# The rotary key's block as fp32 matmuls of 32 columns, and 32 bytes more ahead of the stage tensors

## The reference

```python
h = rmsnorm(x, norm_g)                       # x * rsqrt(mean(x*x)) * gain
proj = h @ w_in
(a_b, a_c, a_x, a_z, c_q, c_kv, k_pe, b_z, dq, dk, dv, c_z, gate_pre) = jnp.split(proj, ...)
q  = rmsnorm(c_q, q_a_norm_g) @ w_uq         # c_q 256 columns
kv = rmsnorm(c_kv, kv_a_norm_g) @ w_ukv      # c_kv 128 columns
k  = concat([k_nope, broadcast(k_pe)])       # k_pe: the rotary key, 32 columns
```

## Time and profile before

| | |
|---|---|
| runs, median (lowest, highest) | 1454.65 us (1454.61, 1457.88) |
| profiled execution, its span | 1454.06 us, 1452.3 us |
| PE, PEld busy | 1438.2 us (99%), 1362.6 us (94%) |
| DVE, ACT, POOL busy | 1043.4 us (72%), 852.3 us (59%), 89.7 us (6%) |
| granted clock of TensorE, mean | 0.999 |
| DMA | 291.93 MB, mean 201 GB/s |

### The profile page before, as it was taken

How to read it: one execution, slowest core, us unless ns; L and a number is a source line. 1 busy time by engine, 2 the same in 40 slices (tenths; PEclk the granted TensorE clock), 3 DMA queues, 4 the chain that set the end, 5 groups by cost and what they waited for, 6 DMA issues and landing times.

```text
span 1452.3 us, 30492 instructions
## 1 busy us (share of the span) xinstructions
PE 1438.2 (99%) x11788; PEld 1362.6 (94%) x11788; DVE 1043.4 (72%) x1781; ACT 852.3 (59%) x1482; POOL 89.7 (6%) x144
## 2 busy tenths in 40 slices
PE   8999999999999999999999999999999999999999
PEld 6888999999989999999998989899999898989999
DVE  2888898987685677865675857876676685787664
ACT  4566666555556666545566776665566576665553
POOL 0111011110000000000001000220000100031000
PEclk9999999999999999999999999999999999999999
DMA  9976699996674465766563555336666355434563
GB/s 364 332 215 213 233 333 335 341 342 224 203 231 152 141 193 184 234 193 193 186 225 121 166 160 160 114 122 188 192 193 217 104 173 167 153 105 141 184 197 116
DMA packets 81122, 291.93 MB, mean 201 GB/s; under 512 B 9185, under 2 KB 10465, under 8 KB 80882
## 3 DMA queue, kind: packets, MB, share of 16 engines
q1 hardware_dynamic: 68274, 244.31, 51.3%
q0 software_dynamic: 11728, 42.64, 8.7%
q10 hardware_dynamic: 1008, 3.41, 0.6%
HBM read 289.27 MB, written 1.05 MB: 200 GB/s over the span
## 4 chain that ended last, share of the span: by engine, by line
PE 91%; DVE 4%; ACT 3%; DMA 1%; issue 1%; SPq 0%; DVEq 0%; ACTq 0%
PE G L528 23%; PE G L530 22%; PE G L529 22%; PE G L587 2%; PE G L589 2%; PE G L588 2%; DVE wlo L1735 1%; PE Tp L981 1%; PE O L1139 1%; ACT whi L1201 1%; PE Tp L923 1%; DMA raw<-in_w 1%; PE S L1105 1%; PE S L1034 1%; DVE aw L1743 1%
## 5 line engine op out<-in xcount | busy, mean ns | idle before, releaser
L1735 DVE TENSOR_TENSOR wlo<-raw,whi 128x1024 fp32r<-128x1024 f32 x444 | 544.1, 1228 | 256.3 <-ACT whi L1201 255.1
L1201 ACT ACTIVATE whi<-raw 128x1024 fp32r<-128x1024 f32 x444 | 468.7, 1058 | 222.0 <-PE G L530 168.2
L528 PE MATMUL G<-h,whi 128*128 128x256 f32 x2064 | 582.7, 282 | 0.3 <-DVE wlo L1735 0.2
L529 PE MATMUL G<-h,whi 128*128 128x256 f32 x2064 | 572.0, 277 | 0.0
L530 PE MATMUL G<-h,wlo 128*128 128x256 f32 x2064 | 571.9, 277 | 0.0
L528 PEld LDWEIGHTS G<-h,whi 128*128 128x128 f32 x2064 | 388.3, 188 | 9.6 <-issue 8.4
L529 PEld LDWEIGHTS G<-h,whi 128*128 128x128 f32 x2064 | 388.1, 188 | 0.7 <-issue 0.5
L530 PEld LDWEIGHTS G<-h,wlo 128*128 128x128 f32 x2064 | 387.9, 188 | 0.0
L1743 DVE CUSTOM_DVE_ANT_0 aw<-aw,cs,cols 128x1024 f32<-128x1024 f32 x80 | 101.4, 1279 | 0.0
L528 PE MATMUL G<-ah,whi 128*128 128x256 f32 x352 | 98.5, 280 | 0.0
L529 PE MATMUL G<-ah,whi 128*128 128x256 f32 x352 | 98.5, 280 | 0.0
(11 more groups left out here) (432 smaller groups left out, 2332.2 us busy)
## 6 DMA issues: line engine op xcount, KB each, us to landing
raw<-in_w SPq DMA_DIRECT2D x444, 512.0 KB, 3.9
aw<-in_ada POOLq DMA_DIRECT2D x80, 512.0 KB, 5.3
adaw<-in_ada SPq DMA_DIRECT2D x8, 1024.0 KB, 15.5
sn<-in_uq ACTq DMA_DIRECT2D x2, 768.0 KB, 4.5
x<-in_x SPq DMA_DIRECT2D x1, 1024.0 KB, 5.3
pt<-in_ukv ACTq DMA_DIRECT2D x2, 512.0 KB, 6.1
out<-x SPq DMA_DIRECT2D x4, 256.0 KB, 2.3
dec<-in_dec ACTq DMA_DIRECT2D x1, 512.0 KB, 7.8
```

Source lines behind the costliest of these rows:

```text
L528: pe.matmul(o, wh, mv[:, 0:T], start=(k == 0), stop=False)
L529: pe.matmul(o, wh, mv[:, T:2 * T], start=False, stop=False)
L1201: act.activation(whi[:, s, :], raw[:, s, :], ACT.Copy).then_inc(w_hi, 1)
L1735: dve.tensor_tensor(wlo[:, s, :], raw[:, s, :], whi[:, s, :], ALU.subtract).then_inc(w_lo, 1)
```

## The change

Five edits.

1. Weight blocks 2 and 3 of each hybrid layer change places: block 2 is now k_pe and block 3 is c_kv. The block of k_pe is still fetched whole, 512 KB.
2. ACT and DVE prepare it in another way: ACT copies the 32 used columns of each k tile to `wkp` (128x256), and DVE multiplies by the norm's gains. There is no high and low part.
3. PE computes it in `rotary_block`: eight fp32 matmuls of 32 columns with x itself as moving operand, tile k into partitions 32 (k mod 4) of the result, so in four column groups of the array. It stands between `run_two` and `entry_sums`.
4. The four partial results lie in 128 partitions of `kpT` and are added by `rotary_key`, whose `ident` corner becomes `eye4`, four 32x32 unit matrices one below the other, made once on DVE.
5. `mark` has 40 words, not 32. All that is allotted behind it starts 32 bytes later; so `mh`, `ah`, `yr`, `oh` and `yh` start at multiples of 64, and `cmask`, `ua` and `hpair` no longer do.

```diff
-        mark = sb("mark", [P, HYB_S])
+        mark = sb("mark", [P, 40])
...
+        eye4 = sb("eye4", [P, 32], stack=second)
+        wkp = sb("wkp", [P, T], stack=second)
...
-        kpT = ua[0:32, 2:2 + T]
+        kpT = ua[:, 2:2 + T]
...
+                def rotary_block():
...
+                    b, g = B_HYB + 2, G_HYB + 2
+                    pe.wait_ge(slot_free[(g - 2) % 4], taken(g - 2) + g4)
+                    pe.wait_ge(w_lo, b + 1 + 4 * b4)
+                    for k in range(KT):
+                        c = 32 * (k % 4)
+                        ins = pe.matmul(gslot(g)[c:c + 32, :], wkp[:, 32 * k:32 * k + 32], x[:, k, :],
+                                        start=(k < 4), stop=(k >= 4))
+                    ins.then_inc(blk_done, 1)
...
+                rotary_block()
                 entry_sums()
-                for j in range(2, 8):
+                for j in range(3, 8):
                     block_u(j)
...
-                        ins = pe.matmul(Tp[:, slot, 32 * j:32 * j + 32], kpT[:, j * P:(j + 1) * P], ident[0:32, 0:32],
+                        ins = pe.matmul(Tp[:, slot, 32 * j:32 * j + 32], kpT[:, j * P:(j + 1) * P], eye4[:, :],
...
+                if n in ROTARY:
+                    act.activation(thin(wkp[:, :]), thin_raw(s), ACT.Copy).then_inc(w_hi, 1)
+                    return
...
+                    dve.tensor_tensor(thin(wkp[:, :]), thin(wkp[:, :]), gain.unsqueeze(2).broadcast_to([P, KT, 32]), ALU.mult).then_inc(w_lo, 1)
...
+            chain.link(dve.tensor_reduce(out=eye4[:, :], in_=ident[:, :].rearrange("p (j c) -> p c j", j=4), op=ALU.add,
+                                         axis=AX))
```

More of the change, by code:

```diff
@@ L48 @@
 N_BLOCKS = B_HYB + LAYERS2 * HYB_BLOCKS
+ROTARY = [B_HYB + l * HYB_BLOCKS + 2 for l in range(LAYERS2)]
 G_QKV = 0
@@ L423, in entry_gain, with thin, thin_raw @@
             return cols[:, c:c + 1] if l else gain0[:, k:k + 1]
+        def thin(ap):
+            return ap.rearrange("p (k c) -> p k c", c=32)
+        def thin_raw(s):
+            return raw[:, s, :].rearrange("p (k c) -> p k c", c=P)[:, :, 0:32]
         def first_tile(b):
@@ L1529, in raw_out @@
                     done(j)
-                    dst = cF[:, j, :] if j < 3 else kpT if j == 3 else bz[:, j - 4, :]
+                    dst = (cF[:, 0, :], cF[:, 1, :], kpT, cF[:, 2, :])[j] if j < 4 else bz[:, j - 4, :]
                     src = S[:, 0, 0:T] if j == 1 else gslot(G_HYB + j)
-                    freed(act.activation(dst, src[0:32, :] if j == 3 else src, ACT.Copy), j)
+                    freed(act.activation(dst, src, ACT.Copy), j)
                 def norm_tiles(ks):
@@ L1734, in lo @@
                 dve.wait_ge(w_hi, n + 1 + 4 * r4)
+                if n in ROTARY:
+                    c = C_HYB + LC + L_NORM
+                    gain = cols[:, c:c + KT] if ROTARY.index(n) else gain0
+                    dve.tensor_tensor(thin(wkp[:, :]), thin(wkp[:, :]), gain.unsqueeze(2).broadcast_to([P, KT, 32]), ALU.mult).then_inc(w_lo, 1)
+                    return
                 dve.tensor_tensor(wlo[:, s, :], raw[:, s, :], whi[:, s, :], ALU.subtract).then_inc(w_lo, 1)
@@ L2216, in _ @@
                     dve.wait_ge(slot_free[n % 4], taken(n) + g4)
-                    dst = cF[:, k, :] if k < 3 else kpT
-                    ins = dve.tensor_tensor(dst, dst, rstd[0:32, :] if k == 3 else rstd[:, :], ALU.mult)
+                    dst = (cF[:, 0, :], cF[:, 1, :], kpT, cF[:, 2, :])[k]
+                    ins = dve.tensor_tensor(dst, dst, rstd[:, :], ALU.mult)
                 ins.then_inc(cs_scaled, 1)
@@ L2580, in lay_out @@
         a_b, a_c, a_x, a_z, c_q, c_kv, k_pe, b_z, dq, dk, dv, c_z, gate = (w[:, p:q] for p, q in zip(at[:-1], at[1:]))
-        parts += [blocks(c_q), blocks(c_kv), blocks(np.pad(k_pe, ((0, 0), (0, 96))))]
+        parts += [blocks(c_q), blocks(np.pad(k_pe, ((0, 0), (0, 96)))), blocks(c_kv)]
         parts += [blocks(b_z), blocks(dq, by_tile), blocks(dk, by_tile), token_blocks(dv), blocks(c_z)]
```

## The result

The changed kernel takes 1444.12 us (median of four runs, 1441.61 to 1449.57) against 1454.63 before; ratio 0.9929, interval 0.9909 to 0.995. A second set of six runs gave 1444.63 and 0.9927 (0.9909 to 0.9945). Forecast: 1444.4.

The account below looks back on a forecast made before the run. PE was taken to bound the kernel (busy 1438.2 of 1452.3 us). Terms: -9.9 - 0.7 + 0.3 = -10.3 us, giving 1444.4 us on the median; own range 1441.5 to 1447, with the third and fourth rivals 1440.5 to 1450.0.

Parts of the forecast that it names:

- predicted -9.9 - 0.7: Matmuls on the five moved tensors: 2688 at 3.7 ns less each, 9.9 us, plus 0.7 us on 258-column ones.
- The 0.7 us for matmuls of 258 columns: In `run_unnormed`, 2 x 96 matmuls on slices of `yr` and `ah`: gain of 0 to 0.7 us, taken as 0.7.
- predicted +0.3: Both hybrid entries together: 5.7 us leaving PE paid back as 1.9 us of rotary blocks and about 4 us of waits.
- where X lands: At both entries the rotary block delays the norm's chain: first block on `h` 0.4 us later, then -0.15 in the second layer.
- X: Time of the rotary block's eight fp32 matmuls ahead of the sums, taken as 0.95 us, upper bound 3.3.
- The lower bound of X: Rotary block at its shortest: four rounds of 0.42 / 2, given as 0.86 us.
- My signs of being right: `ah`, `yr`, `mh` windows at 113 to 114 ns; PE waiting at both entries; sums to first `h` block hardly shorter.
- The first: Rival for the five moved tensors: the 32 bytes gain nothing, only the entries change, 1455.5 us; chance 0.13.
- its region: Within the first rival: slow operands lie high in the partition and `h` low, so a memory region would explain them too.
- the single-file column groups: Rival for the rotary block: groups run one after another, 3.3 us, giving 1449.1 or 1460.2 us; chance 0.03.
- The third: Rival for blocks on the moved tensors: DVE's own work turns a third of the gain into waits, 1448 us; chance 0.07.
- The fourth: Rival for the entries: ACT and DVE have more slack, so -3.8 us instead of +0.3, 1440.3 us; chance 0.03.

Follow-up runs that it names:

- e1: The kernel before with only `mark` enlarged to 40 words (edit 5 alone): 1442.05 us, ratio 0.9913.
- e5: The kernel before with `mark` of 48 words, so stage tensors 64 bytes later and still off the multiple of 64: 1455.38 us, ratio 0.999.
- e6: The changed kernel with `h` alone moved 32 bytes off the multiple of 64: 1468.35 us, ratio to the kernel before 1.0076.
- e10: The changed kernel with the rotary block behind the sums and block 4's weight copies ahead of the root: 1438.32 us, ratio to the kernel before 0.987.
- e12: The changed kernel again, unaltered, six more runs: 1444.63 us, ratio to the kernel before 0.9927.
- e9: The changed kernel with the weights `whi` and `wlo` moved 32 bytes off the multiple of 64: 1477.1 us, ratio to the kernel before 1.0134.
- e2: The changed kernel with `mark` back at 32 words (edits 1 to 4 alone): 1455.38 us, ratio to the kernel before 1.0003.
- e7: The changed kernel with all eight fp32 matmuls of the rotary block in one column group: 1449.66 us, ratio to the kernel before 0.9976.
- e4: The changed kernel with block 4's two weight copies moved ahead of the root: 1439.89 us, ratio to the kernel before 0.9892.

## Why the prediction came out right, and what in it was not

**Edit 5, predicted -9.9 - 0.7.** That the start of the moving operand within 64 bytes costs the time holds: e1, e5 and e6 show it with the time and the windows. The size was a little short, in part since 3.7 ns a matmul came from windows whose counts are one or two too high; from start to start the difference is 3.9. Against the profile before, e1's is 2.1 us shorter in each stretch of `ah` (the term had 2.0), 0.9 in each of `mh` (192 x 3.7 = 0.7), and 1.5 in each merge stage (972.93 to 1066.99 before, 965.48 to 1058.06 in e1), where I had 288 x 3.7 = 1.1: the blocks on `h` there got faster too, from 114.0 to 113.3 ns. `yr` and `oh`, 2.1 us in my sum, gave 0.2 each in that profile and up to 1.5 and 0.9 in others (e10). The 0.7 us for matmuls of 258 columns didn't come: their median distance is 120 ns in the profiles of before, e1, e12 and e10 alike. My reading that the moving operand matters was half the rule (e9). By the Trainium skill's 16-byte line (SBUF — State Buffer, Specifications (TRN2)), as the prediction read it, e1, e5, e6 and e9 would all be at the pace of the kernel they start from. Only e5 is; the others are off by 12, 24 and some 30 us, and the runs decide.

**Edits 1 to 4, predicted +0.3.** The step "where X lands" was right in kind and wrong in size. e2 alone costs nothing that can be told from zero, as forecast; e12 less e1 is +2.6 us, with intervals that overlap. So the cost is read from the entries, not from the times. X was 1.00 (0.95 predicted), and the first of the sums behind it took 0.54 us to the next line's start in place of 0.43, so the chain starts 1.11 us later. First entry: +0.75 to +0.94, predicted +0.4. PE waited three times, 1.5 us for the evacuation of block 2 first, as I had it, which then didn't decide; block 6 waited for its `wlo` and started 14.06 us after the end of `run_two`, 0.3 later than I had (748.9 - 735.13 = 13.77), and the last two blocks took 5.73 us (5.53 in e12) in place of 5.5. Second entry: -0.15 predicted, +1.7 and +2.0 measured. The wait of 2 us is as worked out (`wlo` of block 4), but behind it the clock was at 1.2 GHz for 3.4 us, in both profiles of the changed kernel, which no term of mine had: four blocks took 12.6 us in place of my 11.0. A wait of that length doesn't always do it. Six profiles have the wait, with 1.9 to 2.0 us of idle time (2.15 to 2.31 from start to start). The drop follows in three, the changed kernel, e12 and e9, and not in e2, e6 and e7; e6 has the longest of the six. What decides is open. e4 takes away wait and drop together and gets 3.6 us. (The lower bound of X, four rounds of 0.42 / 2, comes to 0.84 and not 0.86; nothing hangs on it.)

**The sum** is within 0.3 us of the median by luck, since two errors cancel: edit 5 gave 1 to 2 us more, the entries cost 2 us more. My signs of being right came true in part: `ah` in its first stretch and `mh` at 113 ns and the waits at both entries did; `yr` and the second `ah` at 113 didn't, nor did an unchanged second entry.

**The rivals.** The first (32 bytes do nothing) is refuted by e1, its region by e6, the single-file column groups (second) by e7: 3.57 against 1.00. The third, gains lost to waits on DVE: no, `ah` is full at 59.7 us. The fourth: no, though e10 shows what it was after, a chain short enough that the removed block pays.

## What to carry to other kernels

Where PE bounds a kernel, divide windows with one operand by their count and compare tensors; a difference of 3% between tensors under the same load may be their place in memory, and eight words ahead of them may be worth more than removing matmuls. Move them and look: it is one line. Before putting cheap work ahead of a step on which a chain hangs, ask who hangs on it: ahead of the sums the rotary block cost its length at the first entry (19.79 us; 18.48 behind them, which is no more than the 18.50 of e1 without any of edits 1 to 4), and a wait of PE can cost clock on top. Work of other engines that needs nothing from the step (block 4's copies) belongs ahead of it.

## What the runs showed of the hardware

Fp32r matmuls of 128x256 back to back start every 117 to 120 ns if either the weights or the moving operand starts 32 bytes past a multiple of 64 bytes and the other on one (the kernel before, e2, e5, e6 and e9; none of 44 stretches of 96 matmuls or more is under 117.3, from start to start with pauses left out). With both on a multiple they can start every 113. Both off was not tried.

Aligned operands have a slower pace as well, 117.5 ns, that a stretch can take and keep: in the changed kernel's profile from 564.80 through 728.60, 1392 matmuls over a change of tensor, with the clock at 1.00; in e7's the same two stretches; in e2's the 864 on `h`. The same stretch of the same kernel is at 113 in e12. It isn't rare. Nine kernels have the stage tensors and the weights on the multiple; of their long stretches on these tensors `ah` is at 113 in 16 of 18, `oh` in 7 of 9, `mh` in 6 of 18 and `yr` in 2 of 9, and the rest lie at 116 to 118, some of them a mixture. So the multiple of 64 is needed for the fast pace, in all that was tried, but doesn't ensure it. The slow mode would explain why the runs of the kernel before lie at 1451.4 to 1454.7 or at 1456.9 to 1459.0, and one set had a median of 1457.67; that is argued from e2's profile, since those runs have none. What starts it isn't settled, and I didn't try to break it. It needn't begin with a stretch: `yr` in e1 begins at 113.3 ns from start to start, and after four blocks one start comes 186 ns behind the last, at the beginning of a block; from there on it is 117.8. The windows ahead of that place and behind it:

```profile
496.70:507.50 10.80, 10.80 (x97) 1.00 0.43 138
507.90:541.50 33.60, 33.60 (x288) 1.00 0.73 219
```

In the changed kernel it begins in the same way at 558.65 us, at a block's first matmul (158 ns to the next start), two blocks into the shorter stretch of `h` ahead of the long one. Whether such a short stop is the cause isn't shown: in the first stretch of `mh` in e10 and e12 the pace changes in the middle of a block, behind a distance of 122 to 124 ns. A profile of one run must be checked for this mode before stretches are compared.

Column groups run side by side: eight fp32 matmuls of 32 columns and 256 moving columns take 1.00 us in four groups and 3.57 in one.
